# RWKV-7 recurrence: entries placed singly in a pair's period, half additions in the inverse, and the state's decay on GpSimd

## The chip, the cores and the metric

One core of one Trainium2 chip runs the whole kernel. The metric is the device time of one execution, in microseconds. The kernel before took 2343.24 us, the median of three runs (2341.79 to 2350.36). The engines are PE (TensorE), DVE (VectorE), ACT (ScalarE), POOL (GpSimd) and SP (SyncE, here the queue that issues DMAs). Each runs its own program in order and waits on semaphores for the others.

## What is computed

Two layers on 512 latent and 256 context tokens of width 1024. Layer 0 mixes tokens by a bidirectional RWKV-7, layer 1 by grouped-query attention; each is followed by a SwiGLU feed-forward. Only the recurrence of layer 0 is touched by the change. Per head (16 heads of 64) and direction, the reference is:

```python
def rwkv7_scan(S0, r, decay, k, v, kk, a, reverse):
    def step(S, inp):
        r_t, w_t, k_t, v_t, kk_t, a_t = inp
        sa = jnp.einsum('bhvk,bhk->bhv', S, -kk_t)
        S = (S * w_t[:, :, None, :] + sa[..., None] * (kk_t * a_t)[:, :, None, :]
             + v_t[..., None] * k_t[:, :, None, :])
        return S, jnp.einsum('bhvk,bhk->bhv', S, r_t)
```

It runs over the context first and then, from its last state, over the latents, forwards and backwards; `readout` normalizes the sum of both directions, adds a bonus and multiplies by a gate.

## The kernel before

The function `recurrence` (L909) computes this in chunks of 64 tokens. Two heads share the 128 partitions, so there are 8 **pairs** (index t). The 768 tokens are 12 chunks, and step m of a pair takes one chunk forwards and one backwards (e = 0 and 1). Four steps are a **group** (`Group`, with q = 0 to 3 for its steps and j = 0 to 2 for its place in the pair): 24 groups, 96 steps.

A group needs, ahead of its steps:
- its pair's **features** (names such as `map0`, `sigmoid0`, `scan0`, `kk_scale`, `b_grow0`), 128x768 each, on the engine that `ENGINE` and `READOUT` name. `map` are PE products whose result ACT puts through a sigmoid; `through` and `growth` are ACT exponentials; `kk_root` and `y_root` are ACT square roots; `b_gate`, `k_gate`, `k_sum` and `r_decay` run on POOL, the rest of the elementwise work on DVE.
- `score` (PE, two halves) and `mask` (DVE), `keys` and `values` (PE turns them) with their copies on ACT, `diag` (POOL).
- the **inverse** of a 64x64 triangular matrix for each of 8 (step, direction) in levels 0 to 5. `cut` (POOL, L1907) masks the part of a level, `level0` (DVE) starts. Each level n from 1 on is `t` (PE), `t_copy` (ACT), `y` (PE), `add` (DVE, L1673: the inverse plus y, 128x512), then `flip` (DVE, transposed copy) and `swap` (ACT, the copy on the other 64 partitions) for the next level.

The **chain** of states, 96 times in a row: `rhs` (PE: needs the state), `rhs_copy` (ACT), `u` (PE: needs the finished inverse), `u_copy` (ACT), `products` (PE), `update` (DVE, L1692): new state = old state times the chunk's whole decay (`ends`) plus the product, one instruction per direction. The first step of a pair only copies (L1687). `rhs`, `u` and `products` also issue products of the following step and of the output.

When a pair's steps are done, the readout (`y_copy` to `gated`) runs, and SP's `put` stores it. SP's `load(t)` brings k, r and v and two weight slices of pair t, in eight DMAs of which each is issued when the last has landed (L1325, L1330). It waits first for the features of pair t−2 and for the `values` of that pair's second group (L1320). Its queue is load(t), put(t−3), load(t+1) and so on.

What sets the order: `schedule` walks one list, and each engine's part (`Part`) emits its own instructions from it, so every engine runs strictly in the list's order. `slot(s)` is that list: the chain of group s (C), the inverse of s+1 (B) from level 2 on, and scores and levels 0 and 1 of group s+2 (A); features are hung in by `ahead` and `behind` in the slot of their part of the pair. PE's `work_free` hands out two work banks (`WORK`) in turn: a use waits for the reader of the last but one.

## Time and profile before

| | us |
|---|---|
| median of three runs | 2343.24 |
| span of the profiled execution | 2335.9 |
| PE busy in it | 2058.1 |
| DVE, ACT, POOL busy | 1289.9, 914.4, 445.0 |
| six pairs' periods, 446.0 to 905.4 | 459.4 |

Times within the trace count from its first instruction. A group of instructions shows busy time, mean duration, and the idle time of its engine before it with what ended that. "issue" is idle time that ends by nothing the profile shows. PE's matmul records end when the result is out, so that records overlap.

### The profile page before, as it was taken

How to read it: one execution, taken by the hardware profiler on the slowest of the kernel's cores; microseconds unless marked ns; L12 is line 12 of the kernel's file. 1: busy time of each engine (PE TensorE's matmuls, PEld its weight loads, DVE VectorE, ACT ScalarE, POOL GpSimd, SP SyncE). 2: the span in 40 equal slices, each digit the busy share in tenths (PEclk: the TensorE clock that was granted, in tenths of full speed). 3: DMA queues.
4: the chain of work that ended last, by engine and by line, in shares of the span. 5: the costliest groups of instructions: out<-in, count | busy, mean ns of one | idle time of the engine just before them, and what ended most of it. 6: DMA issues, size and time to landing. Idle time of an engine off the chain costs nothing. (4 is left out here: it accounts for less than half of the span.)

```text
span 2335.9 us, 60167 instructions
## 1 busy us (share of the span) xinstructions
PE 2058.1 (88%) x26295; PEld 1785.7 (76%) x26295; DVE 1289.9 (55%) x1904; ACT 914.4 (39%) x1554; POOL 445.0 (19%) x322
## 2 busy tenths in 40 slices
PE   5798997678877887759899999999897988999998
PEld 3597886567766666749899999999863557888887
DVE  4543424667776768533676756756386534333333
ACT  3322323565556655432532323323333533431321
POOL 0011111655466536401000000001220001000000
PEclk8899997899999989979899999999898998999999
DMA  9676763000110010022222122221210012332332
GB/s 316 203 207 206 212 196 115 25 13 24 33 33 22 15 33 11 5 110 86 64 82 73 55 72 77 68 73 37 69 50 19 1 45 64 99 107 83 98 103 86
DMA packets 222294, 192.06 MB, mean 82 GB/s; under 512 B 11482, under 2 KB 206948, under 8 KB 221540
## 3 DMA queue, kind: packets, MB, share of 16 engines
q1 hardware_dynamic: 222052, 188.44, 26.2%
q8 instruction: 199, 3.26, 0.6%
q14 instruction: 43, 0.35, 0.1%
HBM read 170.60 MB, written 17.83 MB: 81 GB/s over the span
## 5 line engine op out<-in xcount | busy, mean ns | idle before, releaser
L1907 POOL TENSOR_TENSOR lvl<-sc_b,level_mask 128x512 f32<-128x512 f32 x144 | 191.3, 1345 | 193.1 <-DVE sc_b L1661 124.8
L530 DVE TENSOR_TENSOR ffn_lo<-ffn_raw,ffn_hi 128x1024 fp32r<-128x1024 f32 (+1 forms) x58 | 77.5, 1336 | 196.5 <-ACT ffn_hi L525 196.5
L550 PE MATMUL banks<-mix_hi,proj_hi 128*128 128x386 f32 (+1 forms) x432 | 153.1, 354 | 14.4 <-DVE proj_lo L530 14.4
L550 PE MATMUL banks<-operand_hi,ffn_w_hi 128*128 128x384 f32 x464 | 155.9, 336 | 4.4 <-DVE operand_lo L496 4.4
L550 PE MATMUL banks<-operand_lo,ffn_w_hi 128*128 128x384 f32 x464 | 155.7, 336 | 0.0
L550 PE MATMUL banks<-operand_hi,ffn_w_lo 128*128 128x384 f32 x464 | 155.5, 335 | 0.0
L550 PE MATMUL banks<-mix_hi,proj_lo 128*128 128x386 f32 (+1 forms) x432 | 148.3, 343 | 0.0
L550 PE MATMUL banks<-mix_lo,proj_hi 128*128 128x386 f32 (+1 forms) x432 | 148.2, 343 | 0.0
L550 PE MATMUL banks<-operand_hi,ffn_hi 128*128 128x512 f32 x352 | 138.7, 394 | 5.2 <-DVE operand_lo L496 2.8
L420 POOL TENSOR_TENSOR norm_squares<-norm_squares,norm_x 128x768 f32<-128x768 f32 (+1 forms) x18 | 29.8, 1655 | 586.7 <-ACT norm_x L414 586.7
L525 ACT CAST ffn_hi<-ffn_raw 128x1024 fp32r<-128x1024 f32 (+1 forms) x60 | 68.3, 1139 | 183.3 <-PE banks L550 183.0
L550 PE MATMUL banks<-operand_lo,ffn_hi 128*128 128x512 f32 x352 | 138.2, 392 | 0.0
L550 PE MATMUL banks<-operand_hi,ffn_lo 128*128 128x512 f32 x352 | 138.1, 392 | 0.0
L1432 PE MATMUL banks<-inverse_t,lvl 64*64 64x64 f32 x3840 | 93.0, 232 | 40.6 <-issue 17.3
L1673 DVE TENSOR_TENSOR inverse<-banks,inverse 128x512 f32<-128x512 f32 x120 | 82.1, 685 | 72.9 <-PE banks L1445 72.9
L1432 PEld LDWEIGHTS banks<-inverse_t,lvl 64*64 64x64 f32 x3840 | 79.8, 144 | 54.7 <-issue 39.8
L2674 ACT CAST ffn_w_hi<-ffn_raw 128x512 fp32r<-128x512 f32 (+1 forms) x116 | 68.7, 605 | 130.2 <-PE banks L550 130.2
L1818 ACT COPY inverse_swapped<-inverse 64x256 f32<-64x256 f32 x240 | 96.7, 403 | 29.9 <-DVE inverse L1673 24.3
L550 PE MATMUL banks<-ffn_t_hi,ffn_w_hi 128*128 128x384 f32 x320 | 106.9, 334 | 0.0
L550 PE MATMUL banks<-ffn_t_lo,ffn_w_hi 128*128 128x384 f32 x320 | 106.9, 334 | 0.0
L550 PE MATMUL banks<-ffn_t_hi,ffn_w_lo 128*128 128x384 f32 x320 | 106.9, 334 | 0.0
L1442 PE MATMUL banks<-inverse,t_sb 64*64 64x64 f32 x1920 | 86.2, 226 | 22.9 <-issue 17.4
(306 smaller groups left out, 5973.9 us busy)
## 6 DMA issues: line engine op xcount, KB each, us to landing
mod_raw<-in_mod_w SPq DMA_DIRECT2D x96, 512.0 KB, 6.1
ffn_raw<-in_ff_w SPq DMA_DIRECT2D x32, 1024.0 KB, 5.2
ffn_raw<-in_ff_w SPq DMA_DIRECT2D x46, 512.0 KB, 3.8
ffn_raw<-in_ff_w SPq DMA_DIRECT2D x16, 704.0 KB, 4.5
proj_raw<-in_rw_wr SPq DMA_DIRECT2D x8, 512.0 KB, 4.6
proj_raw<-in_rw_wk SPq DMA_DIRECT2D x8, 512.0 KB, 4.5
proj_raw<-in_rw_wv SPq DMA_DIRECT2D x8, 512.0 KB, 4.6
rwkv_out_raw<-in_rw_wo SPq DMA_DIRECT2D x8, 512.0 KB, 3.8
```

The lines of the kernel that those rows point to most:

```text
L420: pool.tensor_tensor(self.pool_sum[:, self.at0:], self.pool_sum[:, self.at0:], self.x[:, s, self.at0:], ALU.add)\
L525: signal(act, self.nc.scalar.copy(self.hi[s][:, 0:k_tiles, :], self.raw[s][:, 0:k_tiles, :]), self.rounded, self.at + n + 1)
L530: signal(eng, eng.tensor_tensor(self.lo[s][:, 0:k_tiles, :], self.raw[s][:, 0:k_tiles, :], self.hi[s][:, 0:k_tiles, :].bitcast(F32), ALU.s ...
L550: mm = pe.matmul(out, a, b, start=(first and n == 0), stop=(last and n == 2), skip_group_check=onto)
L1432: mm = pe.matmul(bank[half(h ^ e), out], lvl[G.parity][n % 2][half(h), w, :], inv_t[G.parity][half(h), w, :], start=True, stop=True)
L1442: pe.matmul(bank[half(h), q * CH:q * CH + CH], t_sb[G.parity][half(h), q, :], inv[G.third][half(h), q, :], start=True, stop=True)
L1673: v.tensor_tensor(y, by_way(work(self.use, "y", G.g, n)), y, ALU.add).then_inc(x_added, 1)
L1818: ins = a.copy(inv_s[G.parity][half(1 - h)], inv[G.third][half(h), GROUP:2 * GROUP, :])
L1907: g.tensor_tensor(lvl[G.parity][n % 2][:].rearrange("p (e q) t -> p e q t", e=2), sc_b[G.third][:, :, :, 0, :].rearrange("p q e t -> p e q ...
L2674: nc.scalar.copy(w_hi[x.n % SLOTS][:, 0:x.k_tiles, :], source(x)).then_inc(rounded, 1)
```

## The change

- `slot(s)` is replaced by `period(pair)`: one list for three slots, in which every entry has a place of its own. `at(n)` is group 3·pair + n. So in period `pair` the chain runs from the last step of group at(−7) over the groups at(−6) and at(−5) to the third step of at(−4). Group at(−7) is the last of pair−3, the others are those of pair−2. Scores of at(−4) stand near its start, of at(−3) near 40% and of at(−2) near 80% of the list. The features of pair `pair` begin in the middle and end in the next period; the readout is that of pair−3. The first pair's features come ahead, in a new order (`FIRST`).
- `add` works on the columns that a level changes: for level n, runs of 2^n columns, every other run, 256 of 512 elements.
- The state's decay moves to POOL: `decay` multiplies both directions of the state by `ends` into `kept` (128x128), and `update` adds the product to it in one instruction, after a wait for `decayed`. The first step of a pair has none.
- `gated` shares its buffer with `y_sq`, so `y_square` waits for the store of the pair before. `flip`, `swap` and `t_copy` wait for products of the group two back, `kk_scale` for two more features, `bonus` for `y_bonus` two pairs back.

The whole list of `period`, read from the diff (name(n) is the call for group at(n), with level, half or step behind the comma; name[k] is the feature of pair+k; three calls that do nothing are left out):

```
t_copy(-6,5) rhs(-7,3) rhs_copy(-7,3) y(-6,5) t_copy(-5,2) u(-7,3) decay(-7,3) k_grow1[-1] cut(-5,4) swap(-5,1)
add(-6,5) score(-4,0) u_copy(-7,3) products(-7,3) through0[-1] mask(-4,0) y_copy[-3] y(-5,2) add(-5,2) score(-4,1)
update(-7,3) rhs(-6,0) cut(-5,3) y_square[-3] y_sum[-3] flip(-5,2) mask(-4,1) a_decay0[-1] b_gate1[-1] rhs_copy(-6,0)
y_root[-3] u(-6,0) u_copy(-6,0) t(-5,3) products(-6,0) keys(-4) swap(-5,2) r_decay1[-1] t_copy(-5,3) update(-6,0)
rhs(-6,1) b_grow1[-1] rhs_copy(-6,1) y_invert[-3] cut(-5,5) y(-5,3) keys_copy(-4) u(-6,1) u_copy(-6,1) add(-5,3)
decay(-6,1) products(-6,1) flip(-5,3) swap(-5,3) t(-5,4) cut(-4,0) diag(-3) level0(-4) update(-6,1) y_spread[-3]
t_copy(-5,4) cut(-4,1) rhs(-6,2) flip(-4,0) decay(-6,2) rhs_copy(-6,2) y(-5,4) swap(-4,0) y_scale[-3] add(-5,4)
u(-6,2) t(-4,1) flip(-5,4) u_copy(-6,2) products(-6,2) diag(-2) update(-6,2) t_copy(-4,1) t(-5,5) cut(-4,2) y(-4,1)
y_bonus[-3] add(-4,1) t_copy(-5,5) swap(-5,4) rhs(-6,3) gate[-3] bonus_sum[-1] decay(-6,3) rhs_copy(-6,3) flip(-4,1)
gated[-3] u(-6,3) t(-4,2) swap(-4,1) bonus[-1] u_copy(-6,3) cut(-4,3) products(-6,3) t_copy(-4,2) kk_square[0]
r_decay0[-1] cut(-4,4) update(-6,3) decay(-5,0) y(-5,5) rhs(-5,0) add(-5,5) rhs_copy(-5,0) y(-4,2) a_decay1[-1]
add(-4,2) map0[0] u(-5,0) score(-3,0) sigmoid0[0] flip(-4,2) u_copy(-5,0) kk_sum[0] swap(-4,2) mask(-3,0) kk_limit[0]
products(-5,0) update(-5,0) t(-4,3) kk_root[0] score(-3,1) t_copy(-4,3) decay(-5,1) map2[0] sigmoid2[0] rhs(-5,1)
rhs_copy(-5,1) mask(-3,1) key_gate0[0] y(-4,3) u(-5,1) keys(-3) add(-4,3) flip(-4,3) cut(-3,0) u_copy(-5,1)
products(-5,1) level0(-3) cut(-3,1) update(-5,1) flip(-3,0) swap(-4,3) t(-4,4) keys_copy(-3) k_gate0[0] t_copy(-4,4)
cut(-3,2) swap(-3,0) rhs(-5,2) rhs_copy(-5,2) t(-3,1) scan0[0] map1[0] t_copy(-3,1) y(-4,4) decay(-5,2) u(-5,2)
sigmoid1[0] u_copy(-5,2) kk_invert[0] y(-3,1) add(-4,4) flip(-4,4) add(-3,1) swap(-4,4) map3[0] products(-5,2)
update(-5,2) cut(-4,5) t(-4,5) swap(-3,1) flip(-3,1) rhs(-5,3) scan1[0] decay(-5,3) sigmoid3[0] t_copy(-4,5)
rhs_copy(-5,3) t(-3,2) t_copy(-3,2) cut(-3,3) kk_spread[0] u(-5,3) key_gate1[0] kk_scale[0] u_copy(-5,3) y(-4,5)
products(-5,3) y(-3,2) add(-4,5) score(-2,0) growth0[0] update(-5,3) add(-3,2) rhs(-4,0) swap(-3,2) flip(-3,2)
cut(-3,4) mask(-2,0) rhs_copy(-4,0) score(-2,1) k_gate1[0] u(-4,0) t(-3,3) k_sum[0] growth1[0] u_copy(-4,0)
decay(-4,0) products(-4,0) mask(-2,1) update(-4,0) values(-3) t_copy(-3,3) cut(-2,0) y(-3,3) rhs(-4,1) cut(-2,1)
decay(-4,1) k_grow0[0] values_copy(-3) add(-3,3) keys(-2) flip(-3,3) rhs_copy(-4,1) swap(-3,3) u(-4,1) b_gate0[0]
t(-3,4) u_copy(-4,1) level0(-2) products(-4,1) flip(-2,0) cut(-3,5) keys_copy(-2) cut(-2,2) t_copy(-3,4) t(-2,1)
update(-4,1) swap(-2,0) y(-3,4) b_grow0[0] t_copy(-2,1) add(-3,4) rhs(-4,2) y(-2,1) flip(-3,4) rhs_copy(-4,2)
decay(-4,2) through1[0] add(-2,1) u(-4,2) values(-2) u_copy(-4,2) flip(-2,1) products(-4,2) update(-4,2)
values_copy(-2) t(-3,5) swap(-3,4) t(-2,2) bonus_product[0] diag(-1)
```

The diff, cut to its core:

```diff
         ends = [sb(f"ends{s}", [P, 2, NCH]) for s in range(2)]
-        y_sb, y_sq, gated = sb("y_sb", [P, TOK]), sb("y_sq", [P, TOK]), sb("gated", [P, TOK])
+        y_sb, y_sq = sb("y_sb", [P, TOK]), sb("y_sq", [P, TOK])
+        gated = y_sq
...
+        def new_columns(units, way, n):
+
+            size = 1 << n
+            return bass.AP(units.tensor, units.offset + size,
+                           [units.ap[0], [way - size, 2], [2 * size, GROUP * CH // (2 * size)], [1, size]])
+
...
+        FIRST = ("map0", "map1", "sigmoid0", "map2", "kk_square", "sigmoid1", "scan0", "map3", "sigmoid2", "key_gate0",
+                 "kk_sum", "scan1", "sigmoid3", "key_gate1", "through0", "k_gate0", "kk_limit", "k_gate1", "through1", "k_sum",
+                 "kk_root", "r_decay0", "bonus_product", "growth1", "kk_invert", "r_decay1", "k_grow1", "growth0", "kk_spread",
+                 "kk_scale", "k_grow0", "b_gate1", "a_decay1", "b_gate0", "b_grow1", "bonus_sum", "a_decay0", "b_grow0",
+                 "bonus")
...
+            def period(pair):
+
+                def at(n):
+                    return Group(PER_PAIR * pair + n) if 0 <= PER_PAIR * pair + n < GROUPS else None
+
+                t_copy(at(-6), 5)
+                rhs(at(-7), 3)
...
+                products(at(-5), 3)
+                y(at(-3), 2)
+                add(at(-4), 5)
+                score(at(-2), 0)
+                feature_of(pair, "growth0")
+                update(at(-5), 3)
+                add(at(-3), 2)
...
                         dve.wait_ge(x_ready, self.use.of("y", G.g, n) + 1)
-                        y = inv[G.third][:].rearrange("p (e q) t -> p e (q t)", e=2)
-                        v.tensor_tensor(y, by_way(work(self.use, "y", G.g, n)), y, ALU.add).then_inc(x_added, 1)
+                        x = new_columns(inv[G.third][:], GROUP * CH, n)
+                        v.tensor_tensor(x, new_columns(work(self.use, "y", G.g, n), 512, n), x, ALU.add).then_inc(x_added, 1)
 
                     def flip(self, G, n):
                         if n == 0:
                             dve.wait_ge(level0_done, G.g + 1)
+                            if G.g >= 2:
+                                dve.wait_ge(t_ready, self.use.of("t", G.g - 2, LEVELS - 1) + 1)
                         else:
...
                     def update(self, G, q):
                         m = G.step(q)
                         dve.wait_ge(s_ready, m + 1)
-                        old, new, bank = state[q % 2], state[1 - q % 2], CHAIN[m % 2]
+                        new, bank = state[1 - q % 2], CHAIN[m % 2][:, 256:384].rearrange("p (e t) -> p e t", t=CH)
                         if G.j == q == 0:
-                            ins = v.tensor_copy(new[:], bank[:, 256:384].rearrange("p (e t) -> p e t", t=CH))
+                            ins = v.tensor_copy(new[:], bank)
                         else:
-                            dve.wait_ge(s_done, m)
-                            for e in range(2):
-                                n = G.chunk(q, e)
-                                ins = v.scalar_tensor_tensor(new[:, e, :], old[:, e, :], ends[G.pair][:, e, n:n + 1],
-                                                             bank[:, 256 + e * CH:256 + e * CH + CH], ALU.mult, ALU.add)
+                            dve.wait_ge(decayed, m - m // NCH)
+                            ins = v.tensor_tensor(new[:], bank, kept[:], ALU.add)
                         ins.then_inc(s_done, 1)
 
                     def feature(self, t, name):
...
                         elif name == "kk_scale":
                             after(dve, use, t, "kk_spread")
-                            after(dve, use, t - 1, "b_gate0", "b_gate1")
+                            after(dve, use, t - 1, "b_gate0", "b_gate1", "a_decay0", "a_decay1")
...
                         elif name == "bonus":
                             after(dve, use, t, "bonus_sum")
+                            after(dve, use, t - 2, "y_bonus")
...
                     def t_copy(self, G, n):
                         act.wait_ge(t_ready, self.use.of("t", G.g, n) + 1)
+                        if n == 1 and G.g >= 2:
+                            act.wait_ge(x_ready, self.use.of("y", G.g - 2, LEVELS - 1) + 1)
...
                         elif name == "y_square":
                             after(act, use, t, "y_copy")
+                            need(act, stored, 16 * t)
...
+                    def decay(self, G, q):
+                        m = G.step(q)
+                        pool.wait_ge(s_done, m)
+                        first, last = G.chunk(q, 0), G.chunk(q, 1)
+                        factor = ends[G.pair][:]
+                        factor = bass.AP(factor.tensor, factor.offset + first, [factor.ap[0], [NCH + last - first, 2], [0, CH]])
+                        g.tensor_tensor(kept[:], state[q % 2][:], factor, ALU.mult).then_inc(decayed, 1)
 
                     def cut(self, G, n):
```

## Rows read from the trace of the kernel before

**Rows 1.** The page: the span; PE busy us, share, instructions.

```profile
span 2335.9 us, 60167 instructions
...
PE 2058.1 (88%) x26295; PEld 1785.7 (76%) x26295; DVE 1289.9 (55%) x1904; ACT 914.4 (39%) x1554; POOL 445.0 (19%) x322
```

**Rows 2.** Timeline of ACT: start, length (us), engine, line, operation, tiles, [idle before].

```profile
446.02 0.27 ACT L1823 COPY rhs<-banks 128x128 f32<-128x128 f32 x1 [0.41 <-PE banks L1476]
...
619.22 0.94 ACT L1836 ACTIVATE tmp<-mix_full,par 128x768 f32<-128x768 f32 x1 [0.73 <-PE banks L1629]
```

**Rows 3.** Busy by stretch: PE, PEld, DVE, ACT, POOL; clock, DMA share, GB/s.

```profile
446.00:905.40 459.40, 368.83 (x13414) 316.96 (x13406) 323.23 (x506) 270.53 (x558) 261.77 (x199) 0.95 0.09 25
595.70:671.40 75.70, 63.14 (x2261) 54.74 (x2259) 53.84 (x86) 45.01 (x94) 43.64 (x34) 0.93 0.09 27
905.40:974.30 68.90, 51.59 (x2260) 46.35 (x2262) 44.58 (x78) 32.88 (x80) 30.53 (x29) 1.00 0.03 10
974.30:1021.60 47.30, 37.27 (x1402) 32.16 (x1394) 23.32 (x49) 18.29 (x52) 8.85 (x7) 0.96 0.04 12
```

**Rows 4.** Timeline of PE, first issues of phases in 596 to 642 us.

```profile
596.87 0.27 PE L1442 MATMUL banks<-inverse,t_sb 64*64 64x64 f32 x2
...
597.36 0.25 PE L1532 MATMUL banks<-rhs,inverse 64*64 64x64 f32 x2
...
619.37 0.22 PE L1445 MATMUL banks<-inverse_swapped,t_sb 64*64 64x64 f32 x1
...
620.27 0.33 PE L1389 MATMUL banks<-ar,b 64*64 64x128 f32 x2 [0.22 <-DVE bonus L1761]
...
641.09 0.33 PE L1572 MATMUL banks<-ident,norm_k 128*64 128x128 f32 x2
```

**Rows 5.** The waits, 446 to 1000 us: total us, times, longest.

```profile
ACT u_sb L1827 <- PE banks L1532: 85.5, 77, 2.7
...
DVE inverse L1673 <- PE banks L1445: 59.9, 60, 3.8
```

**Rows 6.** Groups by line, 595.7 to 671.4: busy us, mean ns, idle before.

```profile
L1673 DVE TENSOR_TENSOR inverse<-banks,inverse 128x512 f32<-128x512 f32 x15 | 10.3, 685 | 7.4 <-PE banks L1445 7.4
...
L1692 DVE SCALAR_TENSOR_TENSOR state<-state,ends,banks 128x64 f32<-128x64 f32 x22 | 5.0, 266 | 5.0 <-PE banks L1547 5.0
...
L1873 ACT ACT_TABLE_LOAD x1 | 1.3, 1283 | 0.0
```

**Rows 7.** Single lines, 446 to 1000 us: durations in ns, min/median/max.

```profile
L1687 DVE COPY state<-banks x8: 279/291/292, 449.5 to 978.0; 128x128 f32<-128x128 f32 x8
...
L1893 POOL TENSOR_TENSOR diag<-ident_heads,ends x42: 606/615/1332, 459.1 to 964.9; 128x256 f32<-128x256 f32 x42
...
L1907 POOL TENSOR_TENSOR lvl<-sc_b,level_mask x134: 1257/1276/2003, 447.0 to 999.5; 128x512 f32<-128x512 f32 x134
...
L1729 DVE TENSOR_TENSOR b<-b,sig x12: 916/1917/2028, 508.7 to 902.2; 128x768 f32<-128x768 f32 x12
...
L1923 POOL TENSOR_TENSOR k<-k,k_pair x6: 1812/1820/3281, 567.9 to 881.0; 128x768 f32<-128x768 f32 x6
```

**Rows 8.** Timeline of DVE: first mask of scores, last two state updates.

```profile
399.11 0.69 DVE L1661 TENSOR_TENSOR sc_b<-banks,score_mask 128x512 f32<-128x512 f32 x1 [1.27 <-PE banks L1392]
...
1018.52 0.47 DVE L1692 SCALAR_TENSOR_TENSOR state<-state,ends,banks 128x64 f32<-128x64 f32 x2 [2.20 <-PE banks L1547]
1021.17 0.47 DVE L1692 SCALAR_TENSOR_TENSOR state<-state,ends,banks 128x64 f32<-128x64 f32 x2 [2.18 <-PE banks L1547]
```

**Rows 9.** DMA issues, 440 to 900: count, size, median us to landing.

```profile
v_pair<-v_all SPq DMA_DIRECT2D x12, 192.0 KB, 3.1
```

**Rows 10.** The waits of the SP queue, 446 to 1000 us.

```profile
SPq L1320 <- PE banks L1419: 241.1, 5, 52.1
```

**Rows 11.** Timeline of SP: first and last issues of one load.

```profile
590.12 0.33 SPq L1325 DMA_DIRECT2D mix_full<-in_rw_w  x1
...
609.02 4.01 SPq L1330 DMA_DIRECT2D v_pair<-v_all  x2
```

More of the change, by code:

```diff
@@ L943, in recurrence @@
         rhs, u_sb = sb("rhs", [P, 2, CH]), sb("u_sb", [P, 2, CH])
-        state = [sb(f"state{q}", [P, 2, CH]) for q in range(2)]
+        state, kept = [sb(f"state{q}", [P, 2, CH]) for q in range(2)], sb("state_kept", [P, 2, CH])
         tables, keep_loaded, masks_loaded, stored = (sem(n) for n in ("head_tables", "keep_loaded", "masks_loaded", "pair_stored"))
@@ L1075, in swap, with following, rhs @@
                     E.swap(G, n)
-            def rhs(G, q, following):
+            def following(G, q):
+                if q < GROUP - 1:
+                    return G, q + 1
+                return (Group(G.g + 1), 0) if G.g + 1 < GROUPS else None
+            def rhs(G, q):
                 if G:
-                    E.rhs(G, q, following)
+                    if G.g == q == 0:
+                        E.early(G)
+                    E.rhs(G, q, following(G, q))
             def rhs_copy(G, q):
@@ L1091, in u_copy, with products, decay @@
                     E.u_copy(G, q)
-            def products(G, q, following):
+            def products(G, q):
                 if G:
-                    E.products(G, q, following)
+                    E.products(G, q, following(G, q))
+            def decay(G, q):
+                if G and not G.j == q == 0:
+                    E.decay(G, q)
             def update(G, q):
@@ L1287, in first, with feature_of @@
-            def first(*names):
-                for name in names:
-                    feature(0, name)
-            first("kk_square", "map0", "map1", "sigmoid0", "sigmoid1", "scan0", "scan1", "map2", "map3", "kk_sum", "kk_limit",
[3 rows of a table removed]
-            for s in range(-2, GROUPS):
-                slot(s)
-            for name in ("y_copy", "y_square", "y_sum", "y_root", "y_invert", "y_spread", "gate", "y_scale", "y_bonus", "gated"):
-                feature(CT - 1, name)
+            def feature_of(t, name):
+                if 0 <= t < CT and not (t == 0 and name in FIRST):
+                    feature(t, name)
@@ L1300, in recurrence @@
+            for name in FIRST:
+                feature(0, name)
+            for pair in range(-16, CT + 4):
+                period(pair)
         class Part:
@@ L1306, in recurrence @@
             t = t_copy = y = add = flip = swap = early = feature = nothing
-            rhs = rhs_copy = u = u_copy = products = update = nothing
+            rhs = rhs_copy = u = u_copy = products = decay = update = nothing
         with nc.Block() as block:
```

443 lines of the change are left out of this document (267 added, 176 removed), and 3 rows, old and new, of the table part.

## The prediction

> **What bounds the kernel now.** I read the page's first two parts, then busy times by stretch, then the waits, then the groups of one pair. The whole core shows PE at 88% of the span [rows 1], but that is a mean over stages. In the recurrence a pair of heads starts with its first copy of the right-hand side: pair 0 at 446.02 [rows 2], pair 6 at 905.4. The stretch between holds six periods in 459.4 us, 76.6 us each. In it PE is busy 368.8 us (80%), DVE 323.2 (70%), ACT 270.5 (59%), POOL 261.8 (57%) [rows 3]: no engine is full. PE's busy time also holds the 0.22 us that a product takes to come out after its last issue: the 32 matmul records of one `y` start at 596.87 and the next phase at 597.36, 0.49 us, where group 5 of the page would count 0.7 [rows 4]. Adding issue times over one pair (15 `t` of 0.50, 15 `y` of 0.49, 6 scores of 0.85, 3 keys of 0.95, 12 steps of 0.45+0.23+0.45, values 1.4, four maps of up to 1.5, two sums, two spreads and one gate of about 1.5, bonus 1.3) gives about 52 us. So PE stands still, or waits in order, for some 24 of 76 us. The waits say for what: nobody's long wait is the bound, each engine waits for PE products a little (ACT 85.5 us for u, DVE 59.9 for y) [rows 5]. PE itself waits for copies, turnings and bank readers in the order written in `slot`. The bound is thus the **order**: four queues that each run strictly as written, and chains of handovers across them.
>
> **The change, part by part.** (1) *DVE's additions.* 15 a pair, 0.685 us each [rows 6], now on 256 of 512 elements. No row has this strided form. A copy of 128x128 from PSUM takes 0.291 [rows 7] and the addition of 512 elements 0.685, so 1.03 ns an element and 0.42 us for 256; the other end is 0.69, if short runs (2 elements at level 1) eat the gain, or above, for which nothing speaks. I take 0.42, since the engine's time grew with elements: −4.0 us of DVE a pair. They stand in the inverse's chain (t, copy, y, add, turn), where five levels each get 0.27 us shorter. (2) *The state's decay.* Two instructions of about 0.27, together 0.47 us [rows 6, 8], become one addition like the 0.29 copy: −0.2 us on each step of the state chain and −2.0 us of DVE a pair. POOL gets 11 multiplications of 128x128 a pair. POOL needs 0.606 us for 256 elements and 1.257 for 512 [rows 7], so 0.28 for 128; a disturbed diagonal took 1.33, the upper end. I put 0.45. This adds a wait: `update` waits for `decayed`, and behind it on DVE are queued the next turning or addition and on PE the next `rhs`. (3) *ACT.* The tables are Sqrt, Sigmoid, Exp. Before, y_root, sigmoid0 and growth0 or through1 load one, 3 loads of 1.283 us a pair; kk_root follows y_root and needs none [rows 6]. Now the order is y_root (Sqrt), sigmoid0 (Sigmoid), kk_root (Sqrt), sigmoid2 (Sigmoid), growth0 (Exp): 5 loads, +2.6 us of ACT a pair. (4) *`gated` shares `y_sq`*, so y_square waits for the store of the pair before; that store is issued at `gated`, a third into the period before: nothing. The new waits in flip, swap and t_copy are for products that stand many entries earlier in every queue: nothing, and if that cover fails each costs what its phase is late. (5) *The order itself.* The period goes from three slots to one list of 268 entries.
>
> For (5) I walked the new list by hand, entry by entry, with each engine starting an entry when it is free and its inputs are there. PE entries take the issue times above and give their result 0.22 us later, a handover takes 0.05, and DVE, ACT and POOL entries take their means [rows 6, 7] with the changes above; a work bank is free when the reader of the last but one use is done. One stretch in full, from the state of step (−5,3), group −5 being the second of the pair in the chain: add(−4,5) ends 45.2 and the update 45.5; rhs(−4,0) can only issue behind score(−2,0), which needed that addition's bank (45.35 to 46.2), so 46.2 to 46.65; ACT has growth0 with its load (44.2 to 46.35) and a swap (to 47.15) in front, so rhs_copy ends 47.4; score(−2,1) holds PE to 47.5; u to 47.7, ready 47.85; growth1 ends 48.25, u_copy 48.5; t(−3,3) ends 48.6, products give the state's part at 48.95; the mask of score(−2,1) holds DVE to 49.4, update 49.7. The decay: POOL has k_gate1 (44.0 to 46.4) and k_sum (to 48.3), decay to 48.75, 0.2 before it is needed. The whole walk has the twelve updates end at 4.6, 8.2, 12.6, 15.9, 21.5, 27.6, 33.9, 40.8, 45.5, 49.7, 54.2 and 58.7, and the period closes at **59.3 us**. Three decays come within 0.5 us of their updates (the last three: 48.8 to 48.95, 52.5 to 52.95, 57.7 to 57.9), the others 1.3 to 5 us ahead.
>
> How far is such a walk from the chip? The same done for two stretches of the kernel before: from `y` at 596.87 to `y` at 619.37 it gives 20.8 where 22.5 passed, and from the score at 620.27 to kk_spread at 641.09 it gives 19.8 where 20.8 passed [rows 4]. Together that is 43.3/40.6 = 1.067. So 59.3 becomes 63.3. Both stretches lie in or beside the period of 75.7 [rows 3]; the mean 76.6 over it is 1.012, which gives 64.1. I add 0.9 for the load of the pair to come (rival C): **65.0 us** a period.
>
> **The sum.** Six periods: 6 × (76.6 − 65.0) = −69.6. Pair 6, whose period has few features, took 68.9, 0.90 of a full one [rows 3]: 58.5, −10.4. Pair 7 took 47.3 [rows 3]; its last four steps ran at 2.66 each with nothing but the chain (DVE 1018.52 to 1021.17) [rows 8]. In the new order its last group's scores come only at that period's start, some 28 us of inverse and then four steps of 2.5, so 41: −6.3. Lead-in: from the first score's masks (399.11) [rows 8] to the first right-hand side (446.02) [rows 2] is 46.9 us; in the walk score(−3,0) issues at 24.4 and rhs_copy starts 5.2 into the next period, 40.1, less 1.1 to the mask, times 1.067, 41.6, less a little for the missing neighbours: −6.4 taken. Sum −92.7. Against the profiled span of 2335.9 that is 2243.2; the median of the runs is 7.3 above that span (2343.24), so **2250.5 us**, −4.0%.
>
> **Where the Trainium skill speaks against it.** Rows first: a load is 1.283 us, and there will be 5 a pair for 3 [rows 6]. In my walk y_root's load ends (6.7) before y_sum is there (6.85), and kk_root's ends 0.4 us after kk_limit, so they cost half a microsecond a period. The Trainium skill, "ScalarE: Activation LUTs", section "Table sets: the hidden batching unit", asks to batch activations by set. By that rule, nothing hiding them, the two extra loads are 2 × 1.283 × 8 = 20.5 us, and the sum would be at most 2271 by it. Second: DVE's `b_grow` (L1729), with two SBUF inputs, takes 0.916 to 2.03 us and POOL's k_gate (L1923) 1.8 to 3.3 [rows 7], the long ones where the two ran at once. The Trainium skill, "SBUF — State Buffer", section "Who interferes with whom", says that a DVE instruction with two SBUF inputs and a GpSimd instruction that reads SBUF hold each other up; the new addition of DVE has one SBUF input, and POOL's decay is a new victim. If each of the three tight decays is caught for 1 us, the period is 3 us longer and the time 2271.
>
> **Rivals.** *B, the queues slip.* The new list is tighter than the old, so that one late entry moves four queues. PE issues 52 of 65 us where it did 52 of 76. A period of 70 instead of 65: +30, and +5 at the ends, 2286. For it: the scores, the sums and the maps already share two work banks with the inverse, and in the walk some ten entries of PE wait for a bank's reader. *C, the load sets the period.* Load(t) may start when the values of the middle group two pairs back are turned, and SP waited 241 us for them in five waits [rows 10], so it starts on that event. It is eight DMAs, each issued when the last has landed, 3.1 us for each of the six large ones [rows 9]. The one from 590.12 issued its last at about 612.7 [rows 11], so it landed at 615.8 and took 25.7 us; kk_square came at 619.22 [rows 2], 3.4 us later. Now the values are turned at 57.8 and kk_square stands at 21.4 of the next period: 22.9 us in the walk, 24.4 stretched. So it is at the edge: between nothing and 1.3 us a period, of which the forecast holds 0.9; if pieces take 0.3 us more each it is 3 us: 2263. *D, as good as the walk.* 61.0 a period: 2225. *E, on the other side: the decay decides.* From the point at which a decay ends after its products, every step waits for POOL, whose entries are 1.3 to 3.3 us long [rows 7], with rhs, the bank order and DVE's turnings behind them. To lose all, the period must pass 77.5 us (92.7 us over 7.4 periods, the last two counted as 0.9 and 0.5), so 11 decays late by 1.1 us each; at 2 us each it is 87, and 2250.5 + 7.4 × 22 = 2413. Against it: POOL is busy 43.6 of 75.7 [rows 3] and gets only 3 to 5 us. *F, the change does not do what it says*: the order only moves the idle time, and what remains are DVE's 6 us a pair half hidden: 2330 to 2343.
>
> **How the numbers follow.** Forecast with its own spread (2238 to 2264) 0.60, B 0.18, C 0.09, D 0.06, F 0.03, E 0.04. If the strided addition costs 0.69 instead of 0.42, 15 × 0.27 at half exposure is 2 us a period, 2263 to 2265, inside. Range 2230 to 2296: it leaves out D's lower part, F and E and the tail of B. About 0.5% is what a measurement of this kernel can tell from no change. Faster by more: A, B, C, D, 0.93; within: 0.03; slower: 0.04.
>
> **What would show it.** Right: the first right-hand-side copies of consecutive pairs 63 to 67 us apart; DVE busy about 47 us a period and POOL 47; additions at 0.42, updates at 0.29, decays at 0.3 to 0.45; five table loads a pair; drain steps of 2.5. Update gaps inside a period in the pattern of the walk, the longest at steps (−5,0) to (−5,2) (6 to 7 us), where the maps stand. Wrong: DVE's `update` waiting for POOL in the waits; kk_square waiting for DMA by over 2 us; a period above 70. The forecast fails most easily in the walk's scale factor, taken from 43 us of a looser order.

## The result and the profile after

The changed kernel takes 2303.97 us (median of four runs, 2298.02 to 2310.59) beside 2342.51 for the kernel before, a ratio of 0.9843 (95% interval 0.9811 to 0.9875). It is faster by 37 us by the ratio and 38.5 by the medians, where 93 were forecast: right in sign, and above the range that was given. The page of the kernel after, beside [rows 1]:

```profile
span 2300.2 us, 60266 instructions
...
PE 2042.9 (89%) x26295; PEld 1770.0 (77%) x26295; DVE 1248.9 (54%) x1816; ACT 931.0 (40%) x1567; POOL 491.1 (21%) x410
...
q8 instruction: 199, 3.26, 0.6%
```

PE issues exactly as many instructions as before, and the kernel moves as many instruction blocks (queue q8: packets, MB, share). The busy times by stretch, columns as in [rows 3]: the six periods, one of them, pair 6, and pair 7 up to its last update:

```profile
435.70:868.30 432.60, 356.64 (x13420) 302.88 (x13420) 294.61 (x440) 284.21 (x569) 301.26 (x265) 0.98 0.09 26
641.10:713.70 72.60, 59.40 (x2256) 50.51 (x2252) 49.84 (x75) 48.08 (x96) 50.45 (x45) 1.00 0.10 28
868.30:936.90 68.60, 49.99 (x2186) 44.77 (x2181) 37.53 (x66) 32.82 (x81) 33.57 (x39) 1.00 0.03 10
...
936.90:988.20 51.30, 40.99 (x1379) 35.76 (x1371) 17.23 (x35) 18.27 (x52) 13.74 (x18) 0.81 0.03 11
```

A period is 72.1 us instead of 76.6 [rows 3]; 65.0 was forecast. Pair 6 takes 68.6 for 68.9, pair 7 some 51 for 47.3. Not all of the 4.5 us need be the change's order and parts: with the same number of records PE is busy for 356.6 us in the six periods and was for 368.8, 2.0 us a period less, at a granted clock of 0.98 for 0.95. No run tells that share from the rest. The start of the first right-hand side and of the first mask, which answer to [rows 2] and [rows 8]:

```profile
435.73 0.27 ACT L1944 COPY rhs<-banks 128x128 f32<-128x128 f32 x1 [2.50 <-PE banks L1593]
...
397.70 0.69 DVE L1778 TENSOR_TENSOR sc_b<-banks,score_mask 128x512 f32<-128x512 f32 x1 [1.24 <-PE banks L1509]
```

The span falls by 35.7 us: 8.9 in the lead-in (38.0 for 46.9 us), 6 × 4.5 = 26.8 in the six periods, 0.3 in pair 6; pair 7 gives back 3.6; 3.3 lie outside these stretches. The groups by line of the period from 641.1, beside [rows 6, 7] (busy us, mean ns, idle before):

```profile
L2026 POOL TENSOR_TENSOR state_kept<-state,ends 128x128 f32<-128x128 f32 x12 | 9.1, 759 | 16.6 <-DVE state L1809 16.6
...
L1790 DVE TENSOR_TENSOR inverse<-banks,inverse 128x256 f32<-128x256 f32 x15 | 6.3, 417 | 10.4 <-PE banks L1562 10.4
...
L1809 DVE TENSOR_TENSOR state<-banks,state_kept 128x128 f32<-128x128 f32 x11 | 3.1, 283 | 3.5 <-PE banks L1664 3.4
```

The parts do what they say. An addition takes 0.42 us, an update 0.28, and the decay waits for the state (16.6 us), not the state for the decay. So the missing 56 us are neither in the size of the parts nor in a wait for POOL. They are in rows that the prediction did not read, in the waits of both kernels (total us, times, longest), here those of after, 436 to 985:

```profile
PEld banks L1549 <- issue: 20.8, 24, 2.4
...
PEld banks L1649 <- issue: 17.3, 30, 2.1
PE banks L1549 <- issue: 17.2, 17, 2.2
...
PEld banks L1559 <- issue: 11.0, 12, 1.3
```

and of before, 446 to 1000:

```profile
PEld banks L1432 <- issue: 31.3, 41, 2.5
...
PEld banks L1442 <- issue: 23.8, 43, 2.0
```

"issue" means that PE stood still and nothing that the profile shows had held it. The timeline of PE after shows such places. Each stands in the middle of a phase whose inputs are all there and which had begun to issue (PEld is the weight load that goes with a product, so one stop can show in a row of PEld and in one of PE):

```profile
652.80 0.22 PE L1649 MATMUL banks<-rhs,inverse 64*64 64x64 f32 x1
654.64 0.27 PE L1649 MATMUL banks<-rhs,inverse 64*64 64x64 f32 x2 [1.63 <-issue]
...
702.71 0.22 PE L1521 MATMUL banks<-diag,b 64*64 64x64 f32 x1
704.39 0.21 PE L1521 MATMUL banks<-diag,b 64*64 64x64 f32 x1 [1.46 <-issue]
...
708.46 0.27 PE L1559 MATMUL banks<-inverse,t_sb 64*64 64x64 f32 x2 [1.22 <-issue]
...
712.14 0.21 PE L1664 MATMUL banks<-u_sb,tok 64*64 64x64 f32 x1 [1.14 <-issue]
```

A `u` issues its first product at 652.80 and its second at 654.64; the four stops lie in four kinds of phase.

**Where the stops stand.** I numbered PE's records (weight loads, products, and the semaphore waits and register operations of its queue, by start) from the first of the recurrence and added up the gaps over 0.2 us between issues by the number's remainder modulo 256. In the six periods of after, one remainder, 132, holds 76.2 us, and the other 255 hold 0.28 us each on average, 1.9 at most. In before it is again 132, with 67.9 us, the others 0.39 and 2.6 at most. The numbers of the four stops shown are 16004, 19076, 19332 and 19588: whole multiples of 256 apart. That is the size of what q8 brings: 3.26 MB in 199 packets is 16.4 KB, so 64 bytes for each of 256 instructions. The kernels below agree: half_b has 6624 PE records fewer, 25.9 blocks of 256, and q8 brings 173 packets, 26 fewer; split_y has 7680 more, 30.0 blocks, and 229 packets, 30 more. Of the eleven stops over 0.7 us between 641 and 722 us, ten end 1.19 to 1.51 us after the end of a q8 transfer and one 1.73. And PE hardly ever passes the place sooner. Of the 106 places in the six periods of after, none is passed less than 1.19 us after the end of a transfer. Of the 1156 in the six periods of all twelve kernels of the table below, two are passed less than 1.16 us after one, and of the 458 stops over 0.55 us there, 455 end 1.16 to 1.6 us after one. The reading of this is that PE runs through a block of 256 instructions and stands until the next is there: 12.7 us a period after, 11.3 before. (The expectations below count by an earlier rule, gaps over 0.55 us that end 1.15 to 1.6 us behind a transfer, which gives 12.4 and 10.8.) The stretches from which the walk's scale was taken held 1.3 us of such stops in 43.3 us (the longest 0.76), where the average over before is 6.4 in 43.3.

### The profile page after: what moved, and what is told of

Its sections match the earlier page's. It is cut to its first block and busy times, and to the rows that moved or that the text cites. A ratio compares the mean times of both kernels' runs of the same rounds, so it can differ in the third digit from the quotient of the medians.

```text
span 2300.2 us, 60266 instructions
## 1 busy us (share of the span) xinstructions
PE 2042.9 (89%) x26295; PEld 1770.0 (77%) x26295; DVE 1248.9 (54%) x1816; ACT 931.0 (40%) x1567; POOL 491.1 (21%) x410
## 3 DMA queue, kind: packets, MB, share of 16 engines
q8 instruction: 199, 3.26, 0.6%
## 5 line engine op out<-in xcount | busy, mean ns | idle before, releaser
L2037 POOL TENSOR_TENSOR lvl<-sc_b,level_mask 128x512 f32<-128x512 f32 x144 | 204.6, 1432 | 90.3 <-PE banks L1549 53.6
L530 DVE TENSOR_TENSOR ffn_lo<-ffn_raw,ffn_hi 128x1024 fp32r<-128x1024 f32 (+1 forms) x58 | 77.5, 1335 | 195.3 <-ACT ffn_hi L525 195.3
L525 ACT CAST ffn_hi<-ffn_raw 128x1024 fp32r<-128x1024 f32 (+1 forms) x60 | 68.3, 1139 | 182.7 <-PE banks L550 182.4
L868 POOL TENSOR_TENSOR mix_lo<-mix_full,mix_hi 128x769 fp32r<-128x769 f32 x24 | 40.6, 1692 | 318.0 <-ACT mix_hi L835 318.0
L550 PEld LDWEIGHTS banks<-mix_hi,proj_hi 128*128 128x128 f32 x432 | 82.6, 191 | 29.7 <-DVE proj_lo L530 14.4
L1939 ACT COPY inverse_swapped<-inverse 64x256 f32<-64x256 f32 x240 | 96.8, 403 | 11.4 <-DVE inverse L1790 6.9
L2971 DVE SCALAR_TENSOR_TENSOR residual_stream<-banks,mod,residual_stream 128x256 f32<-128x256 f32 x144 | 60.8, 477 | 73.4 <-PE banks L550 73.2
```

The lines of the kernel that those rows point to most:

```text
L525: signal(act, self.nc.scalar.copy(self.hi[s][:, 0:k_tiles, :], self.raw[s][:, 0:k_tiles, :]), self.rounded, self.at + n + 1)
L530: signal(eng, eng.tensor_tensor(self.lo[s][:, 0:k_tiles, :], self.raw[s][:, 0:k_tiles, :], self.hi[s][:, 0:k_tiles, :].bitcast(F32), ALU.s ...
L550: mm = pe.matmul(out, a, b, start=(first and n == 0), stop=(last and n == 2), skip_group_check=onto)
L868: signal(pool, nc.gpsimd.tensor_tensor(column(mix_lo[q % 2], k), full[s][:], column(mix_hi[q % 2], k).bitcast(F32), ALU.subtract), mix_res ...
L1939: ins = a.copy(inv_s[G.parity][half(1 - h)], inv[G.third][half(h), GROUP:2 * GROUP, :])
L2037: g.tensor_tensor(lvl[G.parity][n % 2][:].rearrange("p (e q) t -> p e q t", e=2), sc_b[G.third][:, :, :, 0, :].rearrange("p q e t -> p e q ...
```

## The experiments

**Theory 1, instruction supply:** the walk was right, and what it lacked are these stops. **Theory 2, the order:** the new list is late for its own reasons (bank readers, slipping queues), and the stops lie in slack. The period and the stops of every kernel, from its own trace (six periods, us a period; stops at the place found by the count above; weight loads and products of PE per us). Each ratio is to runs of before that were made beside that kernel; their medians are 2333.88 to 2342.51:

| kernel | time, us | ratio to before, 95% | period | stops | records/us |
|---|---|---|---|---|---|
| before | 2342.51 | 1 | 76.6 | 11.3 | 58 |
| after | 2303.97 | 0.984 [0.981, 0.988] | 72.1 | 12.7 | 62 |
| shift_128 | 2315.99 | 0.992 [0.990, 0.994] | 72.5 | 13.4 | 62 |
| split_y | 2439.98 | 1.039 [1.032, 1.047] | 90.9 | 19.2 | 60 |
| half_b | 2250.46 | 0.961 [0.958, 0.965] | 66.4 | 4.8 | 55 |
| half_b_order | 2283.07 | 0.979 [0.977, 0.981] | 68.9 | 3.4 | 53 |
| half_b_old | 2282.73 | 0.977 [0.975, 0.979] | 70.1 | 2.6 | 53 |
| half_after | 2258.47 (one run) | | 67.5 | 1.5 | 40 |
| half_before | 2349.31 (one run) | | 79.3 | 2.5 | 34 |
| order_only | 2309.93 | 0.988 [0.985, 0.991] | 72.7 | 11.4 | 62 |
| parts_old_order | 2337.07 | 0.999 [0.997, 1.001] | 77.5 | 13.6 | 58 |
| batched_sets | 2304.73 | 0.985 [0.981, 0.989] | 73.2 | 13.0 | 61 |

**Do the stops belong to a phase or to a place in the instruction stream?** `shift_128` puts 128 instructions of PE ahead of the recurrence:

```diff
+                pe.wait_ge(tables, 6)
+                for _ in range(32):
+                    pe.matmul(WORK[0][half(0), 0:CH], centre[half(0), :], centre[half(0), :], start=True, stop=True)
                 schedule(Pe())
```

> The changed kernel with 32 small products (128 instructions, about 1 us of PE while it would wait for features anyway) ahead of PE's part of the recurrence, which moves every later instruction by half a block of 256. Theory 1: the stops that stand in the middle of a phase move by 128 instructions in program order, that is to other phases (the first u record of step 37 at 652.8 no longer stops), each still ending 1.2 to 1.6 us after a block's transfer; the sum of them stays within 20% and the time within 15 us either way. Theory 2: the gaps stay at the same entries and the time is the same to 2 us.

Counted from the recurrence's own first instruction, the stops stand at remainder 4, 128 from where they were: from the first right-hand side to the last update 72 gaps over 0.7 us have this remainder, and no other remainder has more than one. Not one is at the place of a stop in after, and 63 of after's 70 have one 128 instructions away. The same stretch of the list as at 702.71 above runs through at 718.8, and the stop comes 128 records later, in the products (timeline of PE, shift_128):

```profile
718.80 0.25 PE L1521 MATMUL banks<-diag,b 64*64 64x64 f32 x2
718.84 0.22 PE L1524 MATMUL banks<-diag,k 64*64 64x64 f32 x2
...
721.67 0.21 PE L1671 MATMUL banks<-sc_b,u_sb 64*64 64x64 f32 x1 [1.47 <-issue]
```

A wait for data, a bank or a semaphore would have stayed with its phase and so moved by 128 in the count; these stops stayed at their place in the whole stream and changed their phase. The median is 12 us above after's (0.992 for 0.984 by the ratios), and the first right-hand side comes 10 us later (445.9 for 435.7).

**Fewer instructions.** `half_after` and `half_before` leave out the second head's products in all of PE's methods from the fifth group on:

```diff
...
-                            for h in range(2):
+                            for h in range(1 if G.g >= 4 else 2):
...
```

> From the fifth group on, PE's recurrence products are done for the first of the two heads only: half of PE's instructions in these phases, every wait, copy, addition and order as in the changed kernel. Theory 1 (instruction supply: PE stands still when a block of 256 of its instructions has not arrived; 71 us of such stops in six periods of the changed kernel): the blocks are half as many, nearly all stops go, a period falls from 72 us to 60 to 63 and the kernel to about 2235 to 2250. Theory 2 (handovers between the engines, which the hand walk counted too cheaply): the order and all handovers stay, only issue times on PE shrink a little, a period of 69 to 71 and 2285 to 2300. Theory 3 (the decay or the table loads on the path): as theory 2.

> The same edit in the kernel before: from the fifth group on, PE's products for the first head only. Theory 1: the stops found there (61 us in six periods) lie partly under waits that stay, so a period falls from 76.6 to 67 to 70, about 2290, by less than in the changed kernel; with both edited the gap between the two orders is 6 to 8 us a period instead of 4.5. Theory 2: 73 to 75 us a period, 2325 to 2335, and the gap between the orders stays at 4.5.

The stops go: none after the first period in half_after. But the granted clock goes too, as the windows of the six periods show (half_after, then half_before):

```profile
439.50:844.40 404.90, 380.33 (x7999) 326.37 (x7997) 288.63 (x440) 280.84 (x568) 304.61 (x264) 0.87 0.09 26
```

```profile
446.50:922.40 475.90, 432.84 (x8058) 380.67 (x8053) 319.41 (x507) 271.17 (x557) 265.16 (x200) 0.74 0.08 23
```

PE is busy for longer with 40% fewer products, since part of them ran at the lower clock. Neither theory's numbers came: half_after stands between them (67.5 us and 2258.47, for 60 to 63 and 2235 to 2250, or 69 to 71 and 2285 to 2300), half_before above both. half_before, slower than before, says nothing on the question, and half_after only that the new list without stops and at a low clock takes 67.5 (67.9 to 68.3 in the periods without any stop, at 0.85 to 0.87).

`half_b` leaves out less, the second head's products of the state chain, of the turned keys and of the values alone (the same edit of the loops, in fewer methods), so that PE stays dense:

> The changed kernel; from the fifth group on the products of the chain, the keys and the values are done for the first head only (504 fewer matmul records of some 2250 a pair, and as many weight loads: 22% fewer instructions on PE), scores and inverse in full. Issue times stay, by the full halving before, where PE's granted clock fell to 0.87 and hid half of the gain. Theory 1 (instruction supply): stops fall from 74 us in six periods to 45 to 58, and the mean period from 72.1 to 69 to 70.5, if the clock stays above 0.95; the kernel at 0.973 to 0.980 of the one before. Theory 2 (handovers): stops are not what counts, the period stays within 0.7 of 72.1.

```profile
436.50:834.80 398.30, 356.37 (x11000) 302.20 (x10998) 295.08 (x440) 281.19 (x568) 302.15 (x264) 0.96 0.09 28
576.70:638.90 62.20, 57.57 (x1756) 49.30 (x1754) 51.53 (x76) 46.88 (x97) 51.06 (x45) 1.00 0.10 31
```

At a clock of 0.96 the period falls to 66.4, and to 62.2 in the one from 576.7, which has 1.8 us of stops; the walk said 59.3. Theory 2's 72.1 is out, and Theory 1 is overshot on all counts: 29 us of stops in the six periods for 45 to 58, 66.4 for 69 to 70.5, 0.961 for 0.973 to 0.980. The stops are 7.9 us a period fewer than in after and the period is 5.7 shorter. A small part of that is not the stops': a `u` takes 0.18 us from its first product to its last for 0.23, by the medians, a `y` 0.48 in both. Here the walk can be laid beside the chip step by step: times between the ends of consecutive state updates, from (−6,0) on, and the stops between them:

| step that ends | −6,1 | −6,2 | −6,3 | −5,0 | −5,1 | −5,2 | −5,3 | −4,0 | −4,1 | −4,2 | −4,3 | next −6,0 | sum |
|---|---|---|---|---|---|---|---|---|---|---|---|---|---|
| walk | 4.4 | 3.3 | 5.6 | 6.1 | 6.3 | 6.9 | 4.7 | 4.2 | 4.5 | 4.5 | 5.2 | 3.6 | 59.3 |
| half_b from 576.7 | 4.7 | 3.2 | 6.2 | 6.2 | 7.4 | 6.8 | 4.8 | 4.1 | 4.4 | 5.3 | 5.0 | 4.0 | 62.1 |
| its stops | 0 | 0 | 0.3 | 0 | 0 | 0 | 0 | 0 | 0.3 | 1.2 | 0 | 0 | 1.8 |
| after from 651.2 | 5.0 | 5.4 | 7.9 | 6.5 | 7.4 | 6.8 | 4.8 | 5.0 | 6.2 | 6.6 | 6.4 | 6.0 | 74.0 |
| its stops | 1.8 | 1.1 | 1.8 | 0 | 0.2 | 0 | 0 | 0.9 | 2.4 | 2.8 | 1.5 | 1.3 | 13.7 |

Over the five periods of after from 508 us on, the 21 steps without a stop over 0.25 us are 7.0 us longer than the walk, all together; the 39 with one are 60.5 us longer and hold 61.2 us of stops. So in the new order a stop costs about its own length, and beside the stops the walk missed 1.4 us a period. half_b's steps with a stop are 13.3 longer for 13.8 of stops. That is Theory 1. Theory 2 has a share in half_b's 42 steps without one: 17.9 us over five periods. Of these 5.5 are at (−5,1), 7.4 us every time for 6.3, in after too: an error of the walk; 7.5 are in three steps of 8 to 10.2 us at (−5,2). These three are the clock's: they are the ones in which it fell, to means of 0.59, 0.79 and 0.58, while the two at 1.00 took 6.8 us, as after's did (half_b, the first and the third of the three):

```profile
667.00:677.00 10.00, 9.95 (x146) 6.34 (x150) 4.69 (x8) 5.02 (x11) 4.14 (x3) 0.59 0.01 2
...
800.40:810.60 10.20, 10.16 (x151) 6.52 (x155) 4.72 (x8) 4.91 (x11) 4.09 (x4) 0.57 0.01 2
```

With the clock at 1.00 throughout, after agrees with the walk more closely still. Its three periods from 503.2 on take 72.0 us each and hold 12.0 of stops, which leaves 60.0 for the walk's 59.3:

```profile
503.20:719.30 216.10, 178.82 (x6778) 151.73 (x6770) 149.65 (x225) 142.53 (x286) 151.28 (x133) 1.00 0.10 28
```

**More instructions.** `split_y` issues every product of `y` as two of 32 columns, 21% more PE instructions for the same numbers:

```diff
-                                pe.matmul(bank[half(h), q * CH:q * CH + CH], t_sb[G.parity][half(h), q, :],
-                                          inv[G.third][half(h), q, :], start=True, stop=True)
+                            for c0 in (0, CH // 2):
+                                part = slice(c0, c0 + CH // 2)
...
+                                    pe.matmul(bank[half(h), q * CH + c0:q * CH + c0 + CH // 2], t_sb[G.parity][half(h), q, :],
+                                              inv[G.third][half(h), q, part], start=True, stop=True)
```

> The changed kernel with each product of y issued as two of 32 columns, same result: 480 more matmul records a pair and as many weight loads, 21% more instructions on PE, the same columns. Theory 1: stops rise from 74 us in six periods to 90 or more and the period by 3 to 5 us on top of what the y phases themselves get longer (to be read from their issue time, 0.49 before); the kernel at 0.995 to 1.01 of the one before. Theory 2: only the longer issue of y counts, 15 phases, of which a third to a half are on the path.

```profile
442.40:987.50 545.10, 444.38 (x16276) 384.46 (x16276) 284.36 (x437) 286.93 (x568) 298.06 (x265) 0.89 0.08 22
```

A `y` takes 0.92 us from its first product to its last, where nothing disturbs it, for 0.48: 15 × 0.44 = 6.6 us a period. The stops grow by 6.5, in sum 13.1; the period grows by 18.8, and the kernel stands at 1.039 where Theory 1 had 0.995 to 1.01. So the direction and about a third of the size are the supply's; 5.7 us are the lower clock (0.89 for 0.98) and the order together, not told apart, and the forecast of 3 to 5 us beside the `y` phases was far too low.

**How much of it is the order's, and how much the parts'?** `order_only` has the new list with the old addition and update, `parts_old_order` the new addition and POOL's decay in the old slots (of order_only's edit, the addition; the update and the missing decay are in the cut part):

```diff
-                        x = new_columns(inv[G.third][:], GROUP * CH, n)
-                        v.tensor_tensor(x, new_columns(work(self.use, "y", G.g, n), 512, n), x, ALU.add).then_inc(x_added, 1)
+                        y = inv[G.third][:].rearrange("p (e q) t -> p e (q t)", e=2)
+                        v.tensor_tensor(y, by_way(work(self.use, "y", G.g, n)), y, ALU.add).then_inc(x_added, 1)
...
```

> The new order with the additions on all columns and the state's decay back on DVE (two instructions a step). It tells the order's share from that of the two smaller parts. Theory 1: DVE has 6 us more a period, of which perhaps a third falls on the path beside PE's stops: a period of 74, 2315. Theory 2 (handovers on the chains set the pace): 15 additions 0.27 longer and 11 updates 0.18 longer all count, 6 us a period, 78 us, 2340, so the order alone would bring nothing.

> The old order with both small parts: additions on the changed columns, and the decay on GpSimd, placed right behind each step's rhs. In the new order the two together brought 0.4% with an uncertainty of as much. Theory 1: DVE is off the path while PE stops for instructions, so they bring 0 to 0.4% here too. Theory 2 (every handover counts): 15 x 0.27 + 11 x 0.18 = 6 us a period, 1.7 to 2%. A third possibility: a decay behind a long GpSimd entry holds the update, since the old list was not made for it, and the kernel is slower than before by up to 1%.

order_only at 72.7 us a period and 2309.93 is below the numbers of both theories: most of the gain comes with the order, 3.9 of the 4.5 us a period and 1.2 of the 1.6% (the intervals of order_only and after overlap). In the old slots the parts bring nothing that can be measured (0.999), though DVE is relieved by 5 us a period, as the windows of the six periods show beside [rows 3] (323.23 there):

```profile
441.40:906.60 465.20, 364.81 (x13412) 313.36 (x13404) 291.94 (x439) 270.44 (x558) 293.82 (x265) 0.96 0.09 25
```

PE's stops are 13.6 us a period for 11.3, so 2.3 of the 5 us came back there; where the rest went the trace does not show. The three `half_b` kernels ask the same with most stops gone; `half_b_old` is the kernel before, `half_b_order` order_only, both with half_b's edit:

> The order and the parts are those of the kernel before; only the second head's products of the state chain, of the turned keys and of the values are left out from the fifth group on, as in half_b. Theory 1 (what PE loses beside its list is the supply of its instructions, in both orders): stops fall from 10.8 us a period to 3 to 6, the period from 76.6 to 69 to 71 us, the time to 2285 to 2300 us, so that half_b (66.4 us, 2250 us) is 3 to 4 us a period shorter than it: little more than the 4.5 us between the whole kernels, because both orders lost about the same to the supply. Theory 2 (the new order loses its gain by its own lateness, the supply is the same burden whatever the order): the old order is loose and gains nothing from less PE work, 75 us a period and 2330 us, and the gap to half_b is 8 us a period or more.

> The new order with the additions and the decay as before (order_only), and the same products left out as in half_b. DVE has some 5 us a period more than in half_b. Theory 1 (the small parts were worth 0.5 us a period in the whole kernel because PE's stops covered DVE's time): with few stops the parts come out, the period is 68 to 69 us for 66.4 in half_b, the time 2262 to 2272 us for 2250. Theory 2 (the parts stand beside the path in this order in any case): 66.4 to 67 us a period and 2250 to 2256 us.

half_b_old came at 70.1 us and 2282.73 (just under Theory 1's 2285), half_b_order at 68.9 us in its trace, inside Theory 1's numbers, but with a median of 2283.07 above its 2272 (the traced run is the fastest of its four, 2273.25). Between half_b and half_b_order lie 2.5 us a period and 1.8% (0.961 for 0.979, intervals apart), where the whole kernels differ by 0.4%. That is not the worth of the parts alone. PE has the same 11000 products in both, but is busy for 368.5 us in half_b_order and 356.4 in half_b, 2.0 us a period, at a clock of 0.92 for 0.96:

```profile
439.50:852.70 413.20, 368.51 (x11000) 315.69 (x11000) 317.39 (x505) 282.55 (x569) 270.06 (x199) 0.92 0.09 27
```

So whether the parts bring more where PE is not short of instructions stays open. half_b and half_b_old can be compared, PE being busy for 356.4 and 356.7 us. New over old is 0.9612/0.9768 = 0.984 here, just as in the whole kernels (3.7 us a period for 4.5): the two kernels carry nearly the same burden of stops, so the stops do not make the true gain of the change small. They make my forecast of it large, which had them on one side only. What the order alone is worth with few stops stays unclear: 1.2 us a period by the traces, nothing by the medians, at a clock of 0.92 in half_b_order's six periods and 0.95 in half_b_old's.

**Are the two more table loads on the path?** `batched_sets` moves `map0` and `sigmoid0` behind `key_gate0`, which leaves 3 loads a pair for 5:

```diff
-                feature_of(pair, "map0")
-                feature_of(pair, "sigmoid0")
...
                 feature_of(pair, "key_gate0")
+                feature_of(pair, "map0")
+                feature_of(pair, "sigmoid0")
```

> The changed kernel with map0 and sigmoid0 moved behind key_gate0, so that kk_root follows y_root with no sigmoid between: three table loads a pair as in the kernel before, 2.57 us of ScalarE less a pair. If the loads lie on the path as the rule of batching says, 6 x 2.57 = 15 us and more, 0.977 of the kernel before. Theory 1: ScalarE waits for PE in most places, so 0 to 5 us, 0.982 to 0.985; the moved map may cost a little where it now stands.

2304.73 for 2303.97: no difference. The 15 us of the rule would be 0.977, outside the interval (0.981 to 0.989), so the two loads do not lie on the path at their length; a few us could hide in it.

## Why the prediction was right in sign and wrong in size

- **The step that failed is the scale factor, and with it the period's term of the sum.** The walk's 59.3 was multiplied by 1.067, to stand for what the chip adds to a walk. The 43.3 us from which it was taken held 1.3 us of stops and, in each of the two stretches, 3.4 us at the lower clock (from 599.0 and from 626.3; granted 0.92); the walk has neither. What the chip added in the new order was 12.7 us of stops a period: 59.3 + 12.7 = 72.0, and 72.1 was measured where 65.0 was forecast. That close a sum is in part luck, since the six periods run from 67.5 (the first) to 76.4 (the last, at a clock of 0.93); at full clock it is 60.0 + 12.0. The term was −69.6 and came as −26.8. The comparison was uneven: 76.6 is measured, stops included, and 65.0 is worked out, stops left out. Less the stops, before is 65.3 and after 59.4, a difference of 5.9, in which the clock has its share; with the stops left in, 4.5.
- **What bounds the kernel.** I found that PE issues for 52 of 76 us and gave the other 24 to the order. 11.3 of them are these stops. The waits of before had them in plain sight, as "issue" under more than ten lines of PE; I took the waits that name an engine.
- **Pair 6** (−10.4, came −0.3): the same step, as it was scaled by the same factor. It has 18.4 us of stops for 15.9 before: fewer features, denser PE.
- **Pair 7** (−6.3, came +3.6). Its last four steps were to take 2.5 us each, as 2.66 before [rows 8] (which only the last three took; the one ahead took 4.0). And 28 us of inverse and four steps of 2.5 are 38, not the 41 of the sum:

```profile
980.42 0.29 DVE L1809 TENSOR_TENSOR state<-banks,state_kept 128x128 f32<-128x128 f32 x1 [3.36 <-PE banks L1664]
984.07 0.29 DVE L1809 TENSOR_TENSOR state<-banks,state_kept 128x128 f32<-128x128 f32 x1 [3.36 <-PE banks L1664]
```

  They took 2.8, 3.65, 3.65 and 3.45. This is the clock, granted at 1.00 near the end of before:

```profile
1010.00:1021.00 11.00, 7.21 (x248) 5.79 (x249) 2.11 (x7) 2.12 (x8) 0.00 (x0) 1.00 0.01 3
```

  and at 0.50, the lower of its two levels (1.2 of 2.4 GHz), near the end of after:

```profile
977.00:988.20 11.20, 8.90 (x172) 7.28 (x168) 0.93 (x4) 1.85 (x7) 1.21 (x3) 0.50 0.01 1
```

  That is 3.5 of the 10 us missed; the rest is stops (6.1 us in this pair) and the inverse of the last group, not told apart.
- **Lead-in** (−6.4, came −8.9): right in sign and, within 2.5 us, in size; it holds 1.8 us of stops, and the walk's 40.1 − 1.1 was nearer than its scaled value.
- **The parts**: addition 0.42 as forecast; update 0.28 to 0.29; decay 0.40 at best and in the median, 0.69 on average with some up to 1.87, where 0.45 was put; five table loads of 1.283. DVE fell from 53.9 to 49.1 a period, 2 more than the 47 forecast, and POOL is busy for 50.2 where 47 was forecast: elementwise work got slower beside the busier POOL (`level0` 0.65 to 2.26 us, median 1.46; before, 1.02). The Trainium skill, "SBUF — State Buffer", section "Who interferes with whom", has a DVE instruction with two SBUF inputs contend with a GpSimd instruction that reads SBUF. `level0` has two, and the trace agrees. The only waits that `level0` ended are 5.0 us of POOL's.
- **Rival B** (queues slip, 70 us, 2286) came nearest in number for another reason: the slip beside the stops is 1.4 us a period.
- **Rival C, the load,** did not come: the load from 639.64 landed at 664.1 and kk_square started at 669.5; the one from 568.2 left 1.8 us, the closest, in the first period, 0.7, and ACT waited for none. The 0.9 us added for it were not there.
- **Rival E, the decay,** did not come: it ended a median of 4.0 us before its update, the tightest 0.1, and no update waited for POOL.
- **Tables.** By the Trainium skill's rule ("ScalarE: Activation LUTs", section "Table sets: the hidden batching unit") the two loads could cost up to 20.5 us. batched_sets takes them away and wins nothing that can be measured, so here the measurement decides: grouping by set is not needed where ACT does not hold up the others.

## What to carry to other kernels

Read the waits that end by "issue" before those that name an engine: on a stream of many short products they can be time of the bound engine that a new order does not give back (11.3 us a period before, 12.7 after). When a change is costed by a walk, the walk must carry the same idle time on both sides, or be compared with before less that idle; and a scale from a short stretch holds only what happened in that stretch. In the old slots, 5 us a period taken off DVE were worth nothing that could be measured, and 22% fewer instructions on PE were worth 2.3% in the kernel before and in the changed one alike (half_b_old beside before, half_b beside after): count instructions, not only their durations. And look at the granted clock of every stretch from which a duration, a scale or a difference of two kernels is taken; here it made up to 2 us a period of PE's busy time.

## What was new about the hardware

- PE stands still at one place in every 256 of its instructions, for up to 2.5 us at once, when it issues densely: 0.64 to 0.77 us per 256 on average in the six kernels at 58 to 62 records a us, 0.18 to 0.33 in the three at 53 to 55 (the table's stops times six over 106 such places, or 87 to 88). The mean density is not all of it: parts_old_order has 0.77 at 58, order_only 0.65 at 62, and split_y 0.89 at 60. That the place and the size of q8's blocks agree, that 1154 of 1156 such places are passed 1.16 us or more after such a transfer and that nearly all stops end by 1.6 us after one, is measured; that a late transfer is the cause is the reading of it, since no run changed the transfers themselves.
- Leaving out half of PE's products made the granted clock fall, from 0.95 to 0.74 in the six periods of the kernel before and from 0.98 to 0.87 in the changed one (one run each), and PE was busy for longer with 40% fewer products: 432.8 us for 368.8, and 380.3 for 356.6.
